# Gate and up projections as seven half-size block products in place of eight, their two 258-column chunks alternating matmul by matmul

## The chip, the cores and the metric

The kernel runs on one core of a Trainium2 chip. The metric is the device time of one execution in microseconds (us), the median of three runs. TensorE (PE) multiplies matrices; PEld are its weight loads. VectorE (DVE), ScalarE (ACT) and GpSimd (POOL) work on tiles in SBUF, DVE and ACT also on the PSUM banks that PE writes, and SyncE (SP) issues DMAs. Engines run by themselves and wait for each other by semaphores.

## The reference, cut to what matters

One decoder layer: 1024 prompt rows behind 16 meta rows and 8 sample rows go through a mixer (attention and a gated linear recurrence), then through the feed-forward part that the change touches. D_MODEL is 1024, D_FF is 2816, float32 throughout.

```
def _ffn(x, w_gate, w_up, w_down, g, b):
    hdn = jax.nn.silu(x @ w_gate) * (x @ w_up)
    return _layer_norm(ALPHA * x + hdn @ w_down, g, b)
```

The meta rows are not among the outputs of the layer, so the feed-forward part runs over 1032 columns (tokens).

## The kernel before

Activations lie transposed: features on the 128 partitions, tokens along the columns. Every product in full precision is made of three passes: a float32 value is held as a high part (fp32r) and a low part (the rest), and high weights times high columns, high times low and low times high are summed in PSUM. x1, the input of the feed-forward part, lies in `xh` and `xl` as 8 tiles of 128 features.

**Groups.** D_FF is cut into 11 groups (`FGROUPS`) of 256 hidden rows, that is two units of 128. Per group six weight panels of 128 x 1024 come by DMA into `raw`: gate and up for unit 0, gate and up for unit 1 (`job` with panels p to p+3), and two for the down product. POOL splits each panel into `wh` (a cast, L733) and `wl` (a subtraction, L735); three panel slots rotate, and a slot may be overwritten when PE begins the next panel (`panel_used`).

**Products.** `job` (L794 to L798) makes one unit of gate or up: three chunks of 344 columns (`BODY`), each in a PSUM bank of its own, 8 feature tiles x 3 passes = 24 matmuls a chunk, 72 a unit, 288 a group. ACT applies SiLU to the gate (L1831) into `sg`, DVE multiplies it by the up product (`hidden`, L2457), ACT copies the result into its high part `hh` (L1837), DVE makes the low part `hl` (L2461). `down` (L1350 to L1355) then adds the group's share of the output: 3 chunks x 8 output tiles x 2 units x 3 passes = 144 matmuls, and DVE adds each of the 24 results into `mixed` (L2489). PE runs the groups one after the other in program order; groups 1 to 9 are a loop, and group 0 (its chunks laid between the end of the first layer norm) and the last group are written out.

**The last group.** It makes its output token by token: `turn_y` transposes `mixed` for a tile of tokens (8 transposes, L1396), ACT copies it out (`y_copy`, L1875), `y_tile` adds the last group's down product for that tile with 512 columns of weights as the moving side (L1420 to L1422), and then DVE sums and takes the moments (`moments`, L2504 to L2509), ACT centres and scales (`deviation`, `centre`, L1886), POOL multiplies by the gain (L754) and, for the first three tiles, adds the shift (L758); DVE shifts the others (`shift`, L2526). Nine turns stand behind chunks of the last group's products, and tiles 0 to 3 of nine are made between its last products. SP loads gain and shift when all nine tiles are copied, and stores each tile when it is shifted; the last store ends the kernel.

Of the kernel before, what the change touches and what calls it, by code (L numbers as in the profile page):

```python
# [14 lines left out]
P = 128  # L15
# [49 lines left out]
PANELS = PAN_FFN + 6 * FGROUPS  # L65
# [163 lines left out]
FFN_PER = [5, 5, 5, 5, 5, 5, 3, 3]  # L229
# [10 lines left out]
GATE_LAST, UP_LAST = [0, 2, 4], [1, 3, 5]  # L240
Y_PAIR = [0, 6, 2, 0, 6, 4, 2, 0, 6]
# [8 lines left out]


def chunk_of(token):
    return next(c for c, (c0, cw) in enumerate(BODY) if token < c0 + cw)
# [8 lines left out]
def build(nc, IN, OUT):  # L262
    es = ExitStack()
    with es:
# [129 lines left out]
        mixed = c("mixed", [P, KT, T])  # L394
        sgb = c("sgb", [P, T])
        ysum = nc.alloc_sbuf_tensor_at("ysum", [P, T], F32, offset=R1 + KT * T * 4)
# [4 lines left out]
        z = region(OHB, 16 * T * 4)  # L401
        hh, hl = z("hh", [P, 2, T], F32R), z("hl", [P, 2, T], F32R)
        sg, hf = z("sg", [P, 2, T]), z("hf", [P, 2, 352])

        wh_end = nc.alloc_sbuf_tensor_at("wh_end", [P, D], F32R, offset=OHB + 2 * size([P, 2, T], F32))
        wl_end = nc.alloc_sbuf_tensor_at("wl_end", [P, D], F32R, offset=R1 + KT * T * 4)
        YTOK = OHB + size([P, 6, T], F32) + size([P, 2, 352], F32)
        y = region(YTOK, OHB + 16 * T * 4 - YTOK)
        ytok, ystat = y("ytok", [P, NT, D]), y("ystat", [P, NT, 12])
        ymv, ysd, yms = y("ymv", [P, NT, 2]), y("ysd", [P, NT]), y("yms", [P, NT])  # L410
        gbc = nc.alloc_sbuf_tensor_at("gbc", [P, 2, D], F32, offset=R1)
# [8 lines left out]
        def wt(buf, slot, k):  # L420
            return buf[:, slot, k * P:(k + 1) * P]

# [19 lines left out]
        def _(sp):  # L442
# [27 lines left out]
            for t in range(NT):  # L470
                rows = P if t < 8 else TAIL + NB
                if t == 0:
                    sp.dma_start(xstage[0:META, 0, :], IN["meta"]).then_inc(sem("x_loaded0"), 16)
                    sp.dma_start(xstage[META:P, 0, :], IN["x_prompt"][0, 0:P - META, :])\
                        .then_inc(sem("x_loaded0"), 16)
                elif t < 8:
                    sp.dma_start(xstage[:, t, :], IN["x_prompt"][0, P * t - META:P * t + P - META, :])\
                        .then_inc(sem(f"x_loaded{t}"), 16)
                else:
                    sp.dma_start(xlast[0:TAIL, :], IN["x_prompt"][0, SEQ - TAIL:SEQ, :])\  # L480
                        .then_inc(sem("x_loaded8"), 16)
                    sp.dma_start(xlast[TAIL:TAIL + NB, :], IN["x_sample"][:, 0, :])\
                        .then_inc(sem("x_loaded8"), 16)
# [178 lines left out]
            with sp.Fori(0, FGROUPS) as g:  # L662
                for m in range(4):
                    panel_free(PAN_FFN + 6 * g + m)
                    columns(m % RING, IN["w_up" if m % 2 else "w_gate"][0], 2 * P * g + P * (m // 2))
                for m in range(2):
                    panel_free(PAN_FFN + 6 * g + 4 + m)
                    slot = (4 + m) % RING
                    dst = raw[:, slot, :].rearrange("p (k n) -> p k n", k=2)
                    src = IN["w_down"][0][bass.ds(2 * P * g, 2 * P), :].rearrange("(k p) n -> p k n", p=P)  # L670
                    halves(slot, [(dst[:, k, :], src[:, k, 512 * m:512 * m + 512]) for k in range(2)])
# [15 lines left out]
        def _(pool):  # L687
# [51 lines left out]
            with pool.Fori(27 // RING, PANELS // RING - 1) as i:  # L739
                for s in range(RING):  # L740
                    split(s, i + raw_use(27 + s) - 27 // RING, RING * i + s, RING * i + s - RING)
            for p in range(PANELS - RING, PANELS - 1):
                split(p % RING, raw_use(p), p, p - RING)
            p = PANELS - 1
            pool.wait_ge(raw_loaded[p % RING], 32 * raw_use(p))
            pool.wait_ge(sem("hidden"), 6 * (FGROUPS - 1) + 3)
            pool.tensor_copy(wh_end[:, :], raw[:, p % RING, :]).then_inc(sem("panel_high"), 1)
            pool.wait_ge(sem("panel_high"), PANELS)
            pool.tensor_tensor(wl_end[:, :], raw[:, p % RING, :], f(wh_end[:, :]), ALU.subtract)\
                .then_inc(sem("panel_split"), 1)  # L750
# [12 lines left out]
        def _(pe):  # L763
# [46 lines left out]
            for t in range(NT):  # L810
                rows = P if t < 8 else TAIL + NB
                pe.wait_ge(sem(f"x_loaded{t}"), 32 if t in (0, 8) else 16)
# [524 lines left out]
            def down(g, p):  # L1337
                pe.wait_ge(sem("panel_split"), p + 5)
                pe.wait_ge(sem("panel_split"), p + 6)
                for c, (c0, cw) in enumerate(BODY):  # L1340
                    pe.wait_ge(sem("hidden_split"), 6 * g + 4 + c)
                    for m in range(KT):
# [3 lines left out]
                        for k in range(2):  # L1346
                            w = tuple(x[:, slot, k * 512 + (m % 4) * P:k * 512 + (m % 4 + 1) * P] for x in (wh, wl))
                            x = [x[:, k, c0:c0 + cw] for x in (hh, hl)]
# [26 lines left out]
            with pe.Fori(0, FGROUPS - 2) as g:  # L1375
                B.loop(g, FFN_PER)
                p = PAN_FFN + 6 + 6 * g
                job(p, 0, A3, ALL8, X8, chunks=BODY)
                job(p + 1, 1, B3, ALL8, X8, chunks=BODY)
                job(p + 2, 2, A3, ALL8, X8, chunks=BODY)  # L1380
                job(p + 3, 0, B3, ALL8, X8, chunks=BODY)
                down(g + 1, p)
                B.end(FGROUPS - 2)


            summed = [B.before(b) for b in range(8)]

            def turn_y(i):
                t0, w = Y_TILES[i]
                if i == 0:  # L1390
                    for b in range(8):
                        pe.wait_ge(bank_free[b], summed[b])
                else:
# [5 lines left out]
            p = PAN_FFN + 6 * (FGROUPS - 1)  # L1399
            job(p, 0, A3, ALL8, X8, after=turn_y, chunks=BODY)  # L1400
            job(p + 1, 1, B3, ALL8, X8, after=lambda c: turn_y(c + 3), chunks=BODY)

            def y_tile(i):
                t0, w = Y_TILES[i]
                b, ahead_ = Y_PAIR[i], pair_ahead(i)
                if b == 6 and ahead_ is None:
                    pe.wait_ge(sem("y_copied"), NT)
                elif ahead_ is None:
                    settled(b)
# [1167 lines left out]
```

## Time and profile before

| | us |
|---|---|
| median of 3 runs (1814.51 to 1818.33) | 1817.17 |
| profiled execution, span from first to last instruction | 1820.0 |
| PE busy in it | 1761.5 (97%) |
| DVE / ACT / POOL busy in it | 703.3 / 371.5 / 513.6 |

The profile is of one execution; the rows name a line of the kernel, an engine, what is written from what, and the shape. Two matmuls of PE overlap in the records (each lasts about twice its distance to the next), so the rate of PE is read from starts, not from durations. The feed-forward part begins at about 1041 us, group 0's down product at 1089 us, the last group at 1722 us.

### The profile page before, as it was taken

To read this page: it belongs to the slowest core of one execution; us is meant where nothing else is said; L and a number is where in the kernel's file an instruction comes from. 1 tells how busy PE (TensorE), PEld (TensorE's weight loads), DVE (VectorE), ACT (ScalarE), POOL (GpSimd) and SP (SyncE) were. 2 spreads that over 40 slices of the span, in tenths; PEclk is the share of its full clock that TensorE was granted. 3 is DMA by queue.
4 is the path that set the end of the run, shared out by engine and by line. 5 is a ranking of instruction groups with operands and counts; after the bars stand their busy time and mean duration, and the time that the engine had idled before them with its cause. 6 is when DMAs were issued, how large, how long until landed. Compare 5 with 4: busy or idle time off the path is not lost.

```text
span 1820.0 us, 29093 instructions
## 1 busy us (share of the span) xinstructions
PE 1761.5 (97%) x11328; PEld 1615.3 (89%) x11328; DVE 703.3 (39%) x1255; ACT 371.5 (20%) x699; POOL 513.6 (28%) x296
## 2 busy tenths in 40 slices
PE   7999999998999999999999999999999999999995
PEld 6967677776877879999999899999999999999994
DVE  4156767541335261111174833313312312322327
ACT  4133232322233231111120640010010010010033
POOL 4210111110212023333353823333333333333325
PEclk9899999998998889999999999999999999999998
DMA  5144434304641122111112211111111111111102
GB/s 158 59 112 131 124 116 145 117 12 128 191 135 27 47 50 56 47 46 46 47 47 58 82 47 47 47 46 46 46 46 46 46 46 47 51 45 48 50 25 93
DMA packets 175297, 127.54 MB, mean 70 GB/s; under 512 B 22362, under 2 KB 148730, under 8 KB 175218
## 3 DMA queue, kind: packets, MB, share of 16 engines
q1 hardware_dynamic: 169586, 125.12, 23.3%
q10 hardware_dynamic: 5632, 1.35, 0.5%
q8 instruction: 52, 0.85, 0.2%
q14 instruction: 27, 0.22, 0.0%
HBM read 116.57 MB, written 9.87 MB: 69 GB/s over the span
## 4 chain that ended last, share of the span: by engine, by line
PE 85%; DVE 7%; DMA 2%; ACT 2%; issue 2%; SPq 2%; POOL 0%; DVEq 0%; ACTq 0%; POOLq 0%
PE psum L794 13%; PE psum L798 13%; PE psum L797 13%; PE psum L1355 4%; PE psum L1354 4%; PE psum L1350 4%; PE psum L855 4%; PE psum L859 4%; PE psum L861 4%; PE psum L1010 3%; PE psum L1303 2%; PE psum L1307 2%; PE psum L1306 2%; PE psum L983 2%; PE psum L939 1%
## 5 line engine op out<-in xcount | busy, mean ns | idle before, releaser
L733 POOL CAST wh<-raw 128x1024 fp32r<-128x1024 f32 x131 | 145.8, 1113 | 1258.9 <-PE psum L855 389.4
L794 PE MATMUL psum<-xh,wh 128*128 128x344 f32 (+1 forms) x1392 | 449.0, 323 | 3.6 <-POOL wl L735 3.4
L797 PE MATMUL psum<-xl,wh 128*128 128x344 f32 (+1 forms) x1392 | 446.2, 321 | 0.0
L798 PE MATMUL psum<-xh,wl 128*128 128x344 f32 (+1 forms) x1392 | 446.2, 321 | 0.0
L735 POOL TENSOR_TENSOR wl<-raw,wh 128x1024 fp32r<-128x1024 f32 x131 | 333.3, 2545 | 10.5
L794 PEld LDWEIGHTS psum<-xh,wh 128*128 128x128 f32 x1392 | 263.5, 189 | 5.3 <-issue 5.3
L797 PEld LDWEIGHTS psum<-xl,wh 128*128 128x128 f32 x1392 | 263.5, 189 | 0.5 <-issue 0.5
L798 PEld LDWEIGHTS psum<-xh,wl 128*128 128x128 f32 x1392 | 263.3, 189 | 0.0
L2457 DVE TENSOR_TENSOR hf<-sg,psum 128x344 f32<-128x344 f32 x66 | 33.8, 513 | 372.8 <-PE psum L798 363.7
L855 PE MATMUL psum<-xh,wh 128*128 128x352 f32 (+1 forms) x480 | 162.8, 339 | 1.5 <-DVE ql L1992 1.5
L859 PE MATMUL psum<-xl,wh 128*128 128x352 f32 (+1 forms) x480 | 161.1, 336 | 0.0
L861 PE MATMUL psum<-xh,wl 128*128 128x352 f32 (+1 forms) x480 | 159.9, 333 | 0.0
L1355 PE MATMUL psum<-hh,wl 128*128 128x344 f32 x480 | 154.0, 321 | 0.0
L1350 PE MATMUL psum<-hh,wh 128*128 128x344 f32 x480 | 153.6, 320 | 0.0
L1354 PE MATMUL psum<-hl,wh 128*128 128x344 f32 x480 | 153.3, 319 | 0.0
L2489 DVE TENSOR_TENSOR mixed<-mixed,psum 128x344 f32<-128x344 f32 x216 | 109.9, 512 | 84.3 <-PE psum L1355 84.3
L1831 ACT ACTIVATE sg<-psum 128x344 f32<-128x344 f32 x66 | 30.1, 458 | 414.9 <-PE psum L798 401.6
L855 PEld LDWEIGHTS psum<-xh,wh 128*128 128x128 f32 x480 | 93.5, 195 | 12.0 <-issue 11.8
L859 PEld LDWEIGHTS psum<-xl,wh 128*128 128x128 f32 x480 | 93.3, 194 | 11.7 <-issue 11.7
L861 PEld LDWEIGHTS psum<-xh,wl 128*128 128x128 f32 x480 | 93.1, 194 | 10.1 <-issue 10.0
L2022 DVE CUSTOM_DVE_ANT_0 psum<-psum,cb 128x512 f32<-128x512 f32 (+5 forms) x120 | 63.6, 571 | 75.5 <-PE psum L943 42.5
L1570 ACT ACTIVATE pt<-psum,negc_tok 128x272 f32<-128x272 f32 (+3 forms) x144 | 61.3, 476 | 150.0 <-PE psum L986 78.8
(332 smaller groups left out, 2702.7 us busy)
## 6 DMA issues: line engine op xcount, KB each, us to landing
raw<-in_w_in SPq DMA_DIRECT2D x86, 256.0 KB, 3.3
parts<-in_cache_k SPq DMA_DIRECT2D x64, 256.0 KB, 3.0
parts<-in_cache_v SPq DMA_DIRECT2D x64, 256.0 KB, 2.9
raw<-in_w_gate SPq DMA_DIRECT2D x44, 256.0 KB, 3.1
raw<-in_w_up SPq DMA_DIRECT2D x44, 256.0 KB, 3.1
raw<-in_w_down SPq DMA_DIRECT2D x44, 256.0 KB, 2.7
raw<-in_w_o SPq DMA_DIRECT2D x28, 256.0 KB, 3.1
cb<-negc_scratch SPq DMA_DIRECT2D x8, 520.0 KB, 5.4
```

Of the source, the lines that this page charges most:

```text
L733: pool.tensor_copy(wh[:, s, :], raw[:, r, :]).then_inc(sem("panel_high"), 1)
L735: pool.tensor_tensor(wl[:, s, :], raw[:, r, :], f(wh[:, s, :]), ALU.subtract)\
L794: first = mm(out, w[0], x[0], start=(n == 0), stop=False)
L797: mm(out, w[0], x[1], start=False, stop=False)
L798: last = mm(out, w[1], x[0], start=False, stop=(n == len(ks) - 1))
L855: ins = mm(out, wt(wh, slot, k), xh[:, k, c0:c0 + cw], start=(k == 0), stop=False)
L859: mm(out, wt(wh, slot, k), xl[:, k, c0:c0 + cw], start=False, stop=False)
L861: ins = mm(out, wt(wl, slot, k), xh[:, k, c0:c0 + cw], start=False, stop=(k == 7))
L1350: first = mm(out, w[0], x[0], start=(k == 0), stop=False)
L1354: mm(out, w[0], x[1], start=False, stop=False)
L1355: last = mm(out, w[1], x[0], start=False, stop=(k == 1))
L2489: read(b, ve.tensor_tensor(y, y, psum[:, b, 0:cw], ALU.add))
```

## The change

Groups 1 to 10 (group 0 stays as it was) make gate and up by another formula. A group's gate product is a 2 x 2 block product: the weights in quarters of 128 hidden rows by 512 features, a (row 0, first half of the features), b (row 0, second half), c_ and d (row 1), and x1 in quarters of 512 features by 516 tokens. Eight quarter products are replaced by seven, of which four take sums of quarters:

- POOL makes from the raw quarters S1 = c + d, S3 = a - c, S2 = S1 - a and S4 = b - S2, and splits the seven units a, S1, S3, S2, b, d, S4 into high and low as before, now 128 x 512 each, six slots rotating (`room`: unit g waits until PE has done unit g - 6).
- Four sums of x1 quarters are made once, behind group 0's products: `t_make` and `t_low` on DVE, `t_high` on ACT, each 128 x 2064. They lie in `th` and `tl`; the fourth replaces a part of `xh` and `xl`.
- PE runs seven products (`seven`) for gate and seven for up. Each has 4 feature tiles x 3 passes x 2 chunks of 258 columns = 24 matmuls, into two PSUM banks that alternate. A12, A22 and S4 add onto what lies in the banks of A11, S3 and S1.
- ACT copies the banks of A11 and S1 out first (`snaps`); DVE adds the pieces (`combine`) and from them come the four blocks of 128 x 516 of gate and of up. ACT applies SiLU, DVE multiplies (`hid`), ACT makes the high part (`hid_high`), DVE the low one (`hid_low`). The hidden value takes the place of the gate in `sg`; the low part lies in the same place.
- `down_new` keeps 3 chunks of 344 and 144 matmuls. Its first chunk waits for three of the four low blocks. In its last chunk PE waits twice (`bank_full`) for its own matmuls to end before it tells POOL that a unit is done.
- In the last group turns 0 to 5 stand inside the up job's last three products, the other three beside `y_tile` 0 and 1; all nine tiles are made behind the last product.
- The loop of groups 1 to 9 is written out. SP loads quarters and half panels of 256 KB, each when the split that read its place is done.

The core of the diff:

```diff
+A11, S1, S3, S2, A12, A22, S4 = range(7)
+BANKS_OF = {A11: 0, A12: 0, S1: 2, S4: 2, S3: 4, A22: 4, S2: 6}
+DOWN_BANKS = [6, 7, 0, 1, 4, 5, 2, 3]
...
+            def unit_from(g, source):
+                high, lower = unit_of(wh, g), unit_of(wl, g)
+                step(pool.tensor_copy(high, source))
+                pool.tensor_tensor(lower, source, f(high), ALU.subtract).then_inc(sem("panel_split"), 1)
...
+                    room(g + S1)
+                    s1 = unit_of(wlf, g + S1)
+                    step(pool.tensor_tensor(s1, c_, d, ALU.add))
+                    step(pool.tensor_tensor(c_, a, c_, ALU.subtract))
+                    step(pool.tensor_tensor(a, s1, a, ALU.subtract))
+                    unit_from(g + S1, s1)
+                    room(g + S3)
+                    unit_from(g + S3, c_)
...
+                b, begins = BANKS_OF[v], v in (A11, S1, S3, S2)
+                wH, wL = unit_of(wh, g), unit_of(wl, g)
+                for k in range(4):
+                    cols = slice(k * P, k * P + P)
+                    for w, part in ((wH, 0), (wH, 1), (wL, 0)):
+                        for c in range(2):
+                            last = mm(psum[:, b + c, 0:CW], w[:, cols], moving(v, k, c)[part],
+                                      start=(begins and k == 0 and w is wH and part == 0),
+                                      stop=(k == 3 and w is wL), skip_group_check=True)
...
+                pe.wait_ge(sem("snapped"), 2 * j + 1)
+                product(n, job_, A12, turns)
+                if n == 1 and job_ == 0:
+                    pe.wait_ge(sem("x1_split"), 6 + 4)
+                pe.wait_ge(sem("combined"), 4 * j + 2)
+                product(n, job_, A22, turns)
+                pe.wait_ge(sem("snapped"), 2 * j + 2)
+                product(n, job_, S4, turns)
...
+                for c, (c0, cw) in enumerate(BODY):
+                    pe.wait_ge(sem("hidden_split"), 6 + 4 * (n - 1) + (3 if c == 0 else 4))
...
+                            last = mm(out, w[0], x[1], start=False, stop=(k == 1))
+                            if c == 2 and m % 4 == 3 and k == 0:
+                                last.then_inc(sem("unit_done"), 1)
+                        give(b, last)
+                        if c == 2 and m % 4 == 3:
+                            pe.wait_ge(bank_full[b], B.before(b))
+                            pe.sem_inc(sem("unit_done"), 1)
...
+            for n in range(3):
+                t_make(n)
+            t_low(0)
+            t_low(1)
...
+                product_done(n, job_, A22)
+                combine(n, job_, 2, c21, c12, 4)
+                if job_:
+                    dve.wait_ge(sem("combined"), 4 * j + 3)
+                    dve.wait_ge(sem("gate_rest"), 3 * (n - 1) + 2)
+                    hid(block(1, 0), c21)
+                    hid_low(n, 1)
+                    hid_low(n, 2)
...
+            def hid(g_, u_):
+                ve.tensor_tensor(g_, g_, u_, ALU.mult).then_inc(sem("hidden"), 1)
...
+                dve.wait_ge(sem("hidden_high"), 6 + 4 * (n - 1) + x + 1)
+                ve.tensor_tensor(hl[:, u, cols], sg[:, u, cols], f(hh[:, u, cols]), ALU.subtract)\
+                    .then_inc(sem("hidden_split"), 1)
...
+            seven(FGROUPS - 1, 0)
+            seven(FGROUPS - 1, up, turn_y)
+            pe.wait_ge(sem("panel_split"), PANELS + UNITS_A_GROUP * (FGROUPS - 1))
+            turn_y()
             y_tile(0)
+            turn_y()
             y_tile(1)
-            unit(0, UP_LAST[1], 1, (xh, xl))
-            unit(2, GATE_LAST[2], 2, (xh, xl))
-            y_tile(2)
-            y_tile(3)
-            unit(0, UP_LAST[2], 2, (xh, xl))
-            for i in range(4, NT):
+            turn_y()
+            for i in range(2, NT):
```

Three places in the order of the instructions, the semaphores that each instruction waits for in brackets.

TensorE, in the gate and up stage of a group of the loop. Before, the start of one chunk of a unit (`xh`, `xl` the split input, `wh`, `wl` the split weights):

```order
L794 MATMUL psum<-xh,wh 128x344 [waits bank_free3,panel_split]
L797 MATMUL psum<-xl,wh 128x344
L798 MATMUL psum<-xh,wl 128x344
L794 MATMUL psum<-xh,wh 128x344
L797 MATMUL psum<-xl,wh 128x344
L798 MATMUL psum<-xh,wl 128x344
```

Of the change, the end of product A22 of the up job, product S4 up to its second feature tile (x2 are the two chunks):

```order
L1527 MATMUL psum<-xh,wl 128x258 x2
L1527 MATMUL psum<-xh,wh 128x258 x2
L1527 MATMUL psum<-xl,wh 128x258 x2
L1527 MATMUL psum<-xh,wl 128x258 x2
L1527 MATMUL psum<-xh,wh 128x258 [waits panel_split,snapped]
L1527 MATMUL psum<-xh,wh 128x258
L1527 MATMUL psum<-xl,wh 128x258 x2
L1527 MATMUL psum<-xh,wl 128x258 x2
```

The same weights are now used by two matmuls in a row, on 258 columns each in place of 344; the sequence of high and low is the same, and each product waits for what an earlier piece of its bank was read for.

GpSimd, the weights. Before, the body of the loop, a rotation of three panels:

```order
L733 CAST wh<-raw 128x1024 [waits panel_used]
L734 REGISTER_ALU
L735 TENSOR_TENSOR wl<-raw,wh 128x1024 [waits panel_high]
L726 ISA
L728 REGISTER_ALU [waits raw_loaded1]
L733 CAST wh<-raw 128x1024 [waits panel_used]
L734 REGISTER_ALU
L735 TENSOR_TENSOR wl<-raw,wh 128x1024 [waits panel_high]
L733 CAST wh<-raw 128x1024 [waits raw_loaded2,panel_used]
L734 REGISTER_ALU
L735 TENSOR_TENSOR wl<-raw,wh 128x1024 [waits panel_high]
```

Of the change, the last down unit of group 1 and the first two units of group 2's gate job (`wlf` is the place of a low part, seen as float32, where a sum is made):

```order
L837 CAST wh<-raw 128x512 [waits unit_done,arrived4]
L838 TENSOR_TENSOR wl<-raw,wh 128x512 [waits made]
L837 CAST wh<-raw 128x512 [waits unit_done,arrived0]
L838 TENSOR_TENSOR wl<-raw,wh 128x512 [waits made]
L855 TENSOR_TENSOR wlf<-raw 128x512 [waits unit_done,arrived2,arrived1]
L856 TENSOR_TENSOR raw<-raw 128x512 [waits made]
L857 TENSOR_TENSOR raw<-wlf,raw 128x512 [waits made]
L837 CAST wh<-wlf 128x512 [waits made]
L838 TENSOR_TENSOR wl<-wlf,wh 128x512 [waits made]
```

Between the cast and the subtraction of a panel, which are now half as wide, three sums stand ahead of S1. The first two units of the next group wait for `unit_done` of the running group, that is for its up products A22 and S4.

VectorE, from the up job's first pieces to the start of the down product. Before, the hidden values of the last unit of group 0 (those of the loop read alike):

```order
L2457 TENSOR_TENSOR hf<-sg,psum 128x344 [waits bank_full3,bank_free0]
L2461 TENSOR_TENSOR hl<-hf,hh 128x344 [waits hidden_high]
L2457 TENSOR_TENSOR hf<-sg,psum 128x344 [waits bank_full4,bank_free1]
L2461 TENSOR_TENSOR hl<-hf,hh 128x344 [waits hidden_high]
L2457 TENSOR_TENSOR hf<-sg,psum 128x344 [waits bank_full5,bank_free2]
L2461 TENSOR_TENSOR hl<-hf,hh 128x344 [waits hidden_high]
L2474 SCALAR_TENSOR_TENSOR mixed<-mixed,psum 128x344 [waits bank_full6]
```

Of the change, group 1, `ub` holding the up blocks:

```order
L2790 TENSOR_TENSOR ub<-ub 128x516 [waits snapped,combined]
L2819 TENSOR_TENSOR sg<-sg,ub 128x516 [waits gate_rest,c22_ready]
L2797 TENSOR_TENSOR sg<-sg,psum 128x516 [waits first_read,unit_done]
L2826 TENSOR_TENSOR hl<-sg,hh 128x516 [waits hidden,hidden_high]
L2778 TENSOR_TENSOR ub<-ub,psum 128x516 [waits unit_done]
L2819 TENSOR_TENSOR sg<-sg,ub 128x516 [waits gate_rest,combined]
L2826 TENSOR_TENSOR hl<-sg,hh 128x516 [waits hidden_high] x2
L2778 TENSOR_TENSOR ub<-ub,psum 128x516 [waits unit_done]
L2819 TENSOR_TENSOR sg<-sg,ub 128x516 [waits gate_rest,combined]
L2826 TENSOR_TENSOR hl<-sg,hh 128x516 [waits hidden_high]
L2839 TENSOR_TENSOR mixed<-mixed,psum 128x344 [waits bank_full6]
```

Where a hidden value took the up product from PSUM, three of four now take it from `ub` in SBUF (L2819). The third low block of L2826 is the one that the down product's first chunk waits for.

## Rows read from the trace of the kernel before

**Rows 1.** The page, busy time of each engine.
```profile
PE 1761.5 (97%) x11328; PEld 1615.3 (89%) x11328; DVE 703.3 (39%) x1255; ACT 371.5 (20%) x699; POOL 513.6 (28%) x296
```

**Rows 2.** One line of the down product: count, durations, first and last start.
```profile
L1350 PE MATMUL psum<-hh,wh x480: 316/321/324, 1089.0 to 1721.7; 128*128 128x344 f32 x160
```

**Rows 3.** Timeline of TensorE: start, duration (us), instruction; four widths, three stretches.
```profile
52.13 0.25 PE L877 MATMUL psum<-xh,wl 128*128 128x8 f32 x1
...
54.14 0.25 PE L877 MATMUL psum<-xh,wl 128*128 128x8 f32 x1
...
217.22 0.29 PE L983 MATMUL psum<-ql,kh 64*128 64x256 f32 x2
...
217.45 0.29 PE L986 MATMUL psum<-nmT,onesr 64*128 64x256 f32 x2
...
227.01 0.29 PE L983 MATMUL psum<-ql,kh 64*128 64x272 f32 x2
...
227.26 0.29 PE L986 MATMUL psum<-nmT,onesr 64*128 64x272 f32 x2
...
1764.10 0.39 PE L1421 MATMUL psum<-wh,hl 128*128 128x512 f32 x1
...
1769.20 0.40 PE L1422 MATMUL psum<-wl_end,hh 128*128 128x512 f32 x1
```

**Rows 4.** Timeline of VectorE and TensorE where one waited for the other.
```profile
1774.55 2.42 DVE L2461 TENSOR_TENSOR hl<-hf,hh 128x344 fp32r<-128x344 f32 x1 [0.56 <-ACT hh L1837]
1776.81 0.31 PE L1307 MATMUL psum<-xh,wl 128*128 128x344 f32 x1
1777.11 0.47 PE L1420 MATMUL psum<-wh,hh 128*128 128x512 f32 x1
1777.42 0.40 PE L1421 MATMUL psum<-wh,hl 128*128 128x512 f32 x1
```

**Rows 5.** Timeline of VectorE and ScalarE, one hidden chunk in the loop.
```profile
1262.60 0.51 DVE L2457 TENSOR_TENSOR hf<-sg,psum 128x344 f32<-128x344 f32 x1 [14.54 <-PE psum L798]
1263.14 0.49 ACT L1837 ACTIVATE hh<-hf 128x344 fp32r<-128x344 f32 x1 [3.85 <-DVE hf L2457]
1263.67 0.52 DVE L2461 TENSOR_TENSOR hl<-hf,hh 128x344 fp32r<-128x344 f32 x1 [0.56 <-ACT hh L1837]
```

**Rows 6.** Timeline of GpSimd in the loop.
```profile
1259.12 1.04 POOL L733 CAST wh<-raw 128x1024 fp32r<-128x1024 f32 x1 [7.79 <-PE psum L794]
1260.25 2.40 POOL L735 TENSOR_TENSOR wl<-raw,wh 128x1024 fp32r<-128x1024 f32 x1
```

**Rows 7.** Groups by line and shape: a short cast (busy us, mean ns).
```profile
L715 POOL CAST identr<-ident 128x128 fp32r<-128x128 f32 x1 | 0.3, 291 | 0.1
```

**Rows 8.** The chain of waits: start, duration, ScalarE copy of 1376 columns.
```profile
1065.16 1.36 ACT xh L1825
```

**Rows 9.** Timeline of GpSimd and VectorE side by side before the feed-forward part.
```profile
1015.33 3.58 POOL L735 TENSOR_TENSOR wl<-raw,wh 128x1024 fp32r<-128x1024 f32 x1
1017.15 2.14 DVE L2386 TENSOR_TENSOR ysum<-ysum,mixed 128x344 f32<-128x344 f32 x1
```

**Rows 10.** Timeline of GpSimd during group 0.
```profile
1075.71 2.78 POOL L735 TENSOR_TENSOR wl<-raw,wh 128x1024 fp32r<-128x1024 f32 x1
```

**Rows 11.** Timeline of the last group.
```profile
1722.33 0.51 DVE L2489 TENSOR_TENSOR mixed<-mixed,psum 128x344 f32<-128x344 f32 x1 [0.43 <-PE psum L1355]
...
1774.19 2.40 POOL L754 TENSOR_TENSOR ytok<-ytok,gbc 128x1024 f32<-128x1024 f32 x1 [16.42 <-ACT ytok L1886]
...
1802.43 1.20 DVE L2504 TENSOR_TENSOR ytok<-ytok,psum 128x1024 f32<-128x1024 f32 x1
...
1806.52 1.20 DVE L2504 TENSOR_TENSOR ytok<-ytok,psum 128x1024 f32<-128x1024 f32 x1
```

**Rows 12.** The chain of waits: one turn of eight transposes.
```profile
1726.07 0.87 PE psum L1396 x8
```

**Rows 13.** DMA issues: count, KB each, us to landing.
```profile
gbc<-in_ln_b SPq DMA_DIRECT2D x1, 512.0 KB, 4.8
```

More of the change, by code:

```diff
@@ L661, in _ @@
                 columns((PAN_O + n) % RING, IN["w_o"][0], P * (n % 8))
[L662 to L671, printed above, removed]
+            for m in range(4):
+                panel_free(PAN_FFN + m)
+                columns(m % RING, IN["w_up" if m % 2 else "w_gate"][0], P * (m // 2))
@@ L746, in _, with step @@
[L746 to L750, printed above, removed]
+            steps = [14]
+            def step(ins):
+                steps[0] += 1
+                ins.then_inc(made, 1)
+                pool.wait_ge(made, steps[0])
@@ L1374, in _, with moving @@
             down(0, p)
[L1375 to L1383, printed above, removed]
+            up = 1
+            def moving(v, k, c):
+                low_, high = META + CW * c, META + TH + CW * c
+                if v == A11:
+                    return xh[:, k, low_:low_ + CW], xl[:, k, low_:low_ + CW]
+                if v == A12:
+                    return xh[:, 4 + k, low_:low_ + CW], xl[:, 4 + k, low_:low_ + CW]
+                if v == S4:
+                    return xh[:, 4 + k, high:high + CW], xl[:, 4 + k, high:high + CW]
+                if v == A22:
+                    return xh[:, k, high:high + CW], xl[:, k, high:high + CW]
+                t = {S1: 0, S3: 1, S2: 2}[v]
+                return th[:, t, k, CW * c:CW * c + CW], tl[:, t, k, CW * c:CW * c + CW]
@@ new lines, in hid_high @@
+            def hid_high(n, x):
+                u, h = ((1, 1), (0, 0), (1, 0), (0, 1))[x]
+                act.wait_ge(sem("hidden"), 6 + 4 * (n - 1) + x + 1)
+                do(hh[:, u, TH * h:TH * h + TH], block(u, h), ACT.Copy).then_inc(sem("hidden_high"), 1)
+            for n in range(1, FGROUPS - 1):
+                snaps(n, 0)
+                gate_silus(n)
+                snaps(n, 1)
+                for x in range(4):
+                    hid_high(n, x)
+            snaps(FGROUPS - 1, 0)
@@ L1872, in y_copy @@
+            gate_silus(FGROUPS - 1)
+            snaps(FGROUPS - 1, 1)
             def y_copy(i):
@@ L2491, in _ @@
                     settled(b)
-                B.end(FGROUPS - 2)
-            skip(A3)
-            for c in range(3):
-                hidden(FGROUPS - 1, 0, c)
             def moments(i):
```

457 lines of the change are left out of this document (331 added, 126 removed).

## The prediction

> **What bounds the kernel now.** I read the page's busy times first: PE is busy for 1761.5 of the 1820.0 us span [rows 1], so the time is PE's, and what counts is the distance from one matmul to the next and every wait that PE does not have now. Then the first and last start of the down product's line in groups 0 to 9: 1089.0 and 1721.7 us [rows 2]. Between them lie nine whole groups of 432 matmuls and one down product up to its third last matmul, 9 x 432 + 141 = 4029 distances in 632.7 us, that is 157.0 ns each, the waits in it included. At 344 columns nothing stands still: a group is 432 x 157.0 = 67.8 us, of which gate and up take 288 x 157.0 = 45.2 and down 22.6.
>
> **Price of a matmul on 258 columns.** No row has it. Its neighbours, from starts [rows 3]: 8 columns, 18 distances in 2.01 us, 112 ns (from there on a narrower matmul gains nothing); 256 columns, 2 in 0.23 us, 115; 272 columns, 2 in 0.25, 125; 512 columns, 22 in 5.10, 232. A line from 512 through 344 (157) falls by 0.445 ns a column and gives 118.7 at 258; one from 344 through 272 gives 119; 256 itself gives 115. I take 118.5, with ends 112 (the floor) and 125 (the 272 row as it stands). The 256 and 272 rows use 64 partitions, two at a time; that all 128 cost the same is my choice, since 344 columns lie on the same line. Two PSUM banks in turn are in the 256 and 272 rows too.
>
> The Trainium skill, "TensorE: Matmul & The Clock Gate", section "Back-to-back issue gap", puts an isolated matmul's distance at N / 2.4 + 2.5 ns. By that 258 columns would be 110 and 344 columns 146; the trace has 157 and differs, so the sum does not use it; what 110 would make is a rival below.
>
> **The loop, groups 1 to 9.** Gate and up: 14 products x 24 = 336 matmuls x 118.5 = 39.8 us in place of 45.2, a gain of 5.4. Down stays at 22.6. Three things come back.
>
> First, PE waits twice a group for its own matmul to end. A matmul's record lasts 0.31 us from its start [rows 4], 0.15 beyond its turn; after a wait the next started 0.14 us behind the releaser (VectorE's end at 1774.55 + 2.42 = 1776.97 to 1777.11), and its successor came 0.31 behind it where 0.23 is normal [rows 3, 4]. That is 0.15 + 0.14 + 0.08 = 0.4, twice 0.8 us. Ends: 0.2 and 1.5.
>
> Second, the hidden blocks. Now down's first chunk waits for blocks that came out of PE two chunks earlier (48 x 157.0 = 7.5 us); then it waits for the block of A22, with only S4 (24 x 118.5 = 2.84 us) between. Durations at 516 columns: DVE 0.51 at 344 and 1.20 at 1024 [rows 5, 11] give 0.69; ACT 0.49 at 344 and 1.36 at 1376 [rows 5, 8] give 0.63; handing on costs 0.04 (1262.60 + 0.51 to 1263.14 and so on [rows 5]). From A22's last turn: 0.2 until it ends, combine 0.69, multiply 0.69, ACT's high part 0.63, low part 0.69, four handings 0.16, restart of PE 0.2: 3.3 us against 2.84, late by 0.4.
>
> But VectorE and GpSimd stand in each other's way. A DVE operation on 344 columns with both inputs in SBUF, 0.52 us alone [rows 5], took 2.14 and 2.42 us beside a POOL instruction and ended 0.38 us after it both times [rows 4, 9, 11]; the first of these POOL instructions took 3.58 in place of 2.40 [rows 6, 9]. So each waits for the other's whole instruction, and after it the other goes. The multiply and both low parts of this chain have both inputs in SBUF. POOL is there at just this time: its next units wait for the end of A22 and of S4, as the order above shows. A POOL cast of 512 columns is 0.61 (0.29 at 128, 1.04 at 1024 [rows 6, 7]), a sum or subtraction, with the cast's fixed 0.18, 1.29, of which 1.11 shuts VectorE out; VectorE's stream of 0.54 shuts POOL out. With A22's last turn as zero: its end at 0.2 releases DVE's combine and POOL's cast; the multiply streams from 1.07 to 1.62, POOL's subtraction to 2.73, the first low part to 3.27; S4's end at 3.04 has released POOL's first sum, which streams to 4.38; the second low part ends at 4.92, PE goes on at 5.2. Late by 2.4 us where down could start at 2.84. Ends: 0.4 (POOL never in the way) and 4.3 (all three wait for a whole 1.29).
>
> The Trainium skill, "GPSIMD Engine Reference", section "8. Key points", says that GpSimd shares its SBUF interfaces with VectorE and that it contends with VectorE instructions with two SBUF inputs. The trace agrees: 2.14 us for 0.52. By that rule the move of up blocks from PSUM into `ub` exposes the multiply too; without it the wait would be 0.4 and the result rival 1's.
>
> Third, POOL's weights. A group needs 18 casts, 18 subtractions and 8 sums: 18 x 0.61 + 26 x 1.29 = 44.5, with gaps of 0.08 [rows 6] 48 us of a 65 us group, against 6 x 3.5 = 21 now. Units come 2 us apart (S1 6 us), PE eats one in 2.84, and six slots let POOL work ahead from the last down units on. I cost it at nothing beside the chain above: PE's 22.6 us of down, in which only four units are used, hide it. If POOL were a third slower that cover would be gone.
>
> The other new waits are covered: A22 waits for two combines, 0.2 + 1.5 us, behind A12's 2.84; S1 of the up job for one, behind A11's 2.84.
>
> Group of the loop: 39.8 + 22.6 + 0.8 + 2.4 = 65.6, gain 2.2 us, nine times 20.
>
> **Group 0.** The four sums of x1 quarters are 2064 columns: 2.30 us on DVE, of which 2.15 shut POOL out. Three makes and two low parts stand in VectorE's queue in front of the second unit's hidden values, behind which down 0 waits. VectorE is free at 1076.2, POOL's subtraction runs to 1078.5 [rows 10], and a cast and a subtraction of the last panel (0.9 and 2.2 of stream) come between: 1078.5 + 3 x 2.2 + 3.1 + 2 x 2.3 = 1092.8, then multiply, copy and low part of 344 columns 1.6: down starts at 1094.4 in place of 1089.0, 5.4 late. The other make and low parts delay the reading of PSUM by about as much as down 0 allows; I add 0.6. Cost 6, ends 0 (PE finds cover) and 9.
>
> **Last group.** Now from 1722.1 (the last read less its 0.2) to 1820.0: 97.9 us. After: products 39.8, six turns of 0.87 [rows 12] make 45.0; three more turns, two tiles of 12 x 0.232 = 2.8, and about 2.5 of waits for the last block and for ACT's copies: the ninth copy is out at 56. Only then the gain and shift load, 4.8 us [rows 13]: POOL starts at 61, where now it starts at 1774.2, that is 52 [rows 11]. Seven POOL instructions of 2.48 stand before VectorE's first shift: 78.4. From there a shift of 1.2 and two rounds of 4.1 (1802.43 to 1806.52) to the last tile's moments, 87.8, and from these to the end as now, 13.5 us [rows 11]: 101. So the shorter products are eaten here, because no tile is made between them any more: +3, ends -3 and +6.
>
> **Sum.** -20 + 6 + 3 = -11 on the profiled 1820.0: 1809. That execution stands 2.8 us above the median of 1817.2; from the median it is 1806.
>
> **Rivals.**
> 1. VectorE's chain slips past POOL (PE is late by 0.4 only): the loop gains 4.2, -38 + 9 = -29, 1788. For it: POOL's two releases come only just ahead of VectorE's. Against: a POOL instruction is longer than the room between VectorE's. Chance 0.13.
> 2. The chain loses every turn: late by 4.3 or more at the start of each down product, the loop gains 0.3, -3 + 9 = +6, 1823, slower. It decides from 3.4 us on, where 9 x (4.6 - 3.4) is used up by the 9 of group 0 and the last one. For it: low part 0 and the first multiply can also meet POOL; against: the chain above has POOL at its worst in two of three places. Chance 0.15.
> 3. 258 columns cost 125 ns as 272 did: 3360 x 6.5 = 22 us back, 1828, slower. Against: the lines through 344. Chance 0.08.
> 4. They cost 112 or less, the floor of the 8-column row: 3360 x 6.5 = 22 us more, 1784. For it: 256 at 115; against: the lines through 344. Chance 0.10. The skill's 110 of the section named above would make it 1777.
> 5. POOL cannot feed PE: it waits for units in every group, above 1830. Chance 0.04.
>
> **How the numbers follow.** The forecast has 0.50, and its own range, from late 1.5 to 3.2, is 1798 to 1814. What a measurement of this kernel can tell from no change is 0.2%, 3.6 us. Faster: forecast 0.46, rivals 1 and 4 0.23, together 0.69. Slower: most of 2, 3, 5, 0.20. Same 0.11. The range of 8 in 10 leaves out 5, the far end of 4 and most of 3: 1782 to 1826.
>
> **What would show it.** Right: L1527's starts 118 or 119 ns apart; PE's idle time in the loop mainly ahead of L1587's first matmul, some 2.4 us nine times, put down to VectorE's low part L2826, whose mean is well above 0.69; down 0's first start 5 to 6 us after the last chunk; POOL's first gain about 61 us into the last group. Wrong: L1527 above 122; idle PE behind POOL's units; L2826 at 0.69, which is rival 1.

## The result and the profile after

The changed kernel takes 1829.23 us (median of 5 runs, 1823.61 to 1831.73), 1.0065 times the kernel before, with a 95% interval of 1.0046 to 1.0083. It is slower by some 12 us; forecast was 1806, faster by 11. The forecast missed by 23 us. The profiled execution has a span of 1828.0 us, to be held against the 1820.0 of before. PE has 480 matmuls more and is 32.5 us less busy than in [rows 1]:

```profile
PE 1729.0 (95%) x11808; PEld 1579.7 (86%) x11808; DVE 824.2 (45%) x1323; ACT 392.1 (21%) x701; POOL 769.7 (42%) x616
```

So the matmuls did become cheaper, and what was gained stands idle or went elsewhere. By stretches, from starts on PE (before from [rows 2, 11]):

| us | before | forecast | after |
|---|---|---|---|
| up to the last gate or up matmul of group 0 | 1088.8 | 1088.8 | 1083.6 |
| from there to group 1 | 22.8 | 28.8 | 30.0 |
| groups 1 to 9 | 610.4 | 590 | 608.9 |
| last group, to the end | 97.8 | 101 | 105.5 |

The first line is no effect of the change: among the profiled kernels below that have the same code there, that matmul starts between 1081 and 1092 us. Most of the miss is in the loop, which should have given 20 us and gave 1.6.

The waits of PE from 1075 us on (total, times, longest, in us) stand where they were forecast:

```profile
PE psum L1587 <- DVE hl L2826: 18.4, 9, 2.0
PE psum L1475 <- DVE hl L2711: 5.2, 1, 5.2
PE psum L1527 <- PE psum L1589: 2.7, 9, 0.3
```

L1587 is the first matmul of a new down product and L2826 VectorE's low part, L1475 is group 0's down product, L1527 behind L1589 the wait of PE for its own matmul, seen at the end of down only. The timeline of group 1 (start, duration, instruction) shows the first of these waits and what comes after it:

```profile
1152.19 0.69 DVE L2819 TENSOR_TENSOR sg<-sg,ub 128x516 f32<-128x516 f32 x1
...
1152.26 1.78 POOL L838 TENSOR_TENSOR wl<-raw,wh 128x512 fp32r<-128x512 f32 x1
...
1152.81 3.49 DVE L2826 TENSOR_TENSOR hl<-sg,hh 128x516 fp32r<-128x516 f32 x2
...
1153.91 0.40 PE L1527 MATMUL psum<-xh,wl 128*128 128x258 f32 x2
1154.48 1.26 POOL L855 TENSOR_TENSOR wlf<-raw 128x512 f32<-128x512 f32 x1 [0.44 <-PE psum L1527]
...
1156.35 0.43 PE L1587 MATMUL psum<-hh,wh 128*128 128x344 f32 x1 [2.04 <-DVE hl L2826]
1156.61 0.32 PE L1588 MATMUL psum<-hh,wl 128*128 128x344 f32 x1
...
1157.71 0.36 PE L1589 MATMUL psum<-hl,wh 128*128 128x344 f32 x1
1157.87 0.49 PE L1587 MATMUL psum<-hh,wh 128*128 128x344 f32 x1
1158.15 0.49 PE L1588 MATMUL psum<-hh,wl 128*128 128x344 f32 x1
...
1161.02 0.44 PE L1589 MATMUL psum<-hl,wh 128*128 128x344 f32 x1
1161.30 0.33 PE L1587 MATMUL psum<-hh,wh 128*128 128x344 f32 x1
```

Up to 1156.61 this is the forecast: POOL's subtraction and sum stand between VectorE's steps, two low parts need 3.49 us, PE goes on 2.3 us behind the start of its last product matmul. Then comes what no step had: from 1157.87 to 1161.30 twelve matmuls follow each other at 0.286 us in place of 0.157. 12 x 0.13 = 1.5 us are lost after the wait has ended. The view by stretches (length, PE busy, granted clock, then the share and the GB/s of DMA) shows what it is, one row per down product with what separates it from the next group, groups 1, 2, 3 and 9, then group 0:

```profile
1156.35:1181.56 25.21, 24.76 (x145) 0.93 0.04 11
1224.32:1248.05 23.73, 23.27 (x145) 1.00 0.04 12
1290.82:1316.05 25.23, 24.77 (x145) 0.93 0.04 11
...
1698.79:1722.52 23.73, 23.27 (x145) 1.00 0.04 12
1089.13:1113.66 24.53, 24.53 (x144) 0.92 0.01 2
```

At a mean of 0.93 part of the stretch ran at 0.50, the lower level of 1.2 GHz. Seven of the nine groups have 0.93 and 25.2 us, two have 1.00 and 23.7. So a loop group takes 68.0 or 66.5 us, where 67.8 was before and 65.6 forecast.

The last group's chain (start, duration) goes over the load of gain and shift and POOL:

```profile
1779.53 6.57 DMA gbc<-in_ln_b
...
1786.17 2.42 POOL ytok L879
```

At its end VectorE's first shift stands beside one more POOL instruction and takes 3.27 us, where the next one takes 1.20 (timeline):

```profile
1803.04 3.27 DVE L2872 TENSOR_TENSOR ytok<-ytok,gbc 128x1024 f32<-128x1024 f32 x1 [10.03 <-POOL ytok L879]
...
1809.20 1.20 DVE L2872 TENSOR_TENSOR ytok<-ytok,gbc 128x1024 f32<-128x1024 f32 x1
```

### The profile page after: what moved, and what is told of

The parts are those of the page before. It is cut to its first block, busy times and chain, and to the rows that moved or that the text cites. A ratio compares the mean times of both kernels' runs of the same rounds, so it can differ in the third digit from the quotient of the medians.

```text
span 1828.0 us, 29515 instructions
## 1 busy us (share of the span) xinstructions
PE 1729.0 (95%) x11808; PEld 1579.7 (86%) x11808; DVE 824.2 (45%) x1323; ACT 392.1 (21%) x701; POOL 769.7 (42%) x616
## 4 chain that ended last, share of the span: by engine, by line
PE 82%; DVE 10%; issue 2%; DMA 2%; ACT 2%; POOL 1%; SPq 1%; DVEq 0%; ACTq 0%; POOLq 0%
PE psum L1527 21%; PE psum L919 5%; PE psum L922 5%; PE psum L923 5%; PE psum L1587 4%; PE psum L1589 4%; PE psum L1588 4%; PE psum L980 4%; PE psum L984 4%; PE psum L986 4%; PE psum L1135 3%; PE psum L1108 2%; PE psum L1428 2%; PE psum L1432 2%; PE psum L1431 2%
## 5 line engine op out<-in xcount | busy, mean ns | idle before, releaser
L811 POOL TENSOR_TENSOR wl<-raw,wh 128x1024 fp32r<-128x1024 f32 x72 | 191.1, 2654 | 5.8
L838 POOL TENSOR_TENSOR wl<-raw,wh 128x512 fp32r<-128x512 f32 x140 | 185.2, 1323 | 11.2
L1587 PE MATMUL psum<-hh,wh 128*128 128x344 f32 x432 | 144.7, 335 | 19.7 <-DVE hl L2826 18.4
L919 PE MATMUL psum<-xh,wh 128*128 128x344 f32 (+1 forms) x480 | 156.4, 326 | 4.8 <-POOL wl L811 3.4
L923 PE MATMUL psum<-xh,wl 128*128 128x344 f32 (+1 forms) x480 | 155.2, 323 | 0.0
L922 PE MATMUL psum<-xl,wh 128*128 128x344 f32 (+1 forms) x480 | 155.1, 323 | 0.0
L1589 PE MATMUL psum<-hl,wh 128*128 128x344 f32 x432 | 142.9, 331 | 0.0
L1527 PE MATMUL psum<-xh,wh 128*128 128x258 f32 x640 | 130.4, 285 | 2.7 <-PE psum L1589 2.7
L1527 PE MATMUL psum<-xh,wl 128*128 128x258 f32 x640 | 129.1, 283 | 0.0
L1527 PE MATMUL psum<-xl,wh 128*128 128x258 f32 x640 | 129.1, 283 | 0.0
L1587 PEld LDWEIGHTS psum<-hh,wh 128*128 128x128 f32 x432 | 85.1, 197 | 23.9 <-DVE hl L2826 20.2
L980 PEld LDWEIGHTS psum<-xh,wh 128*128 128x128 f32 x480 | 93.3, 194 | 12.0 <-issue 11.8
L1527 PEld LDWEIGHTS psum<-xh,wh 128*128 128x128 f32 x640 | 99.1, 189 | 5.0 <-issue 5.0
L984 PEld LDWEIGHTS psum<-xl,wh 128*128 128x128 f32 x480 | 93.0, 194 | 11.7 <-issue 11.7
```

The costliest lines, as they stand in the source:

```text
L811: pool.tensor_tensor(wl[:, s, :], raw[:, r, :], f(wh[:, s, :]), ALU.subtract)\
L838: pool.tensor_tensor(lower, source, f(high), ALU.subtract).then_inc(sem("panel_split"), 1)
L919: first = mm(out, w[0], x[0], start=(n == 0), stop=False)
L922: mm(out, w[0], x[1], start=False, stop=False)
L923: last = mm(out, w[1], x[0], start=False, stop=(n == len(ks) - 1))
L980: ins = mm(out, wt(wh, slot, k), xh[:, k, c0:c0 + cw], start=(k == 0), stop=False)
```

## The experiments

**The idle time filled.**

```diff
+                    if c == 0:
+                        pe.wait_ge(sem("combined"), 4 * j + 1)
+                        for _ in range(18):
+                            mm(psum[:, 6, 0:CW], xh[:, 0, META:META + P], xh[:, 0, META:META + CW], ...)
                     pe.wait_ge(sem("hidden_split"), 6 + 4 * (n - 1) + (3 if c == 0 else 4))
```

> The changed kernel, with 18 matmuls of 258 columns whose result nobody reads laid ahead of each of the nine new down products, into PSUM bank 6, which stands empty there: 18 x 0.12 = 2.2 us, as long as PE waits at this place in the changed kernel. The wait stays, PE is only not idle in it. Theory 1 (the granted clock falls to its lower level because PE stands idle): no stretch of lower clock in the loop, the down product takes 23.1 us in all nine groups in place of 24.6 in seven of them, 7 x 1.5 = 10.5 us less, 1829 to 1818.5. Rival (the matmuls at double distance after the wait have another cause, such as POOL's or VectorE's traffic): the stretch stays and the time stays at 1829, or rises by what the extra matmuls run over the wait, at most 9 x 0.3.

Measured: 1816.59 us (12 runs), 1.0001 times the kernel before (0.9988 to 1.0014). From the timeline of group 1, and the stretch of its down product with the filling:

```profile
1152.56 2.32 PE L1575 MATMUL psum<-xh 128*128 128x258 f32 x18
1154.79 0.43 PE L1592 MATMUL psum<-hh,wh 128*128 128x344 f32 x1
```
```profile
1152.56:1178.51 25.95, 25.50 (x165) 1.00 0.04 11
```

All nine stretches have 1.00. Down starts no earlier than in the changed kernel, 2.36 us behind the last product matmul, and yet 12.6 us are gone. By the traces 10.3 of them lie in the loop, where 10.5 were expected; the last group is 1.6 us shorter, since its load took 4.87 us in that execution in place of 6.57. The lower clock comes from PE's standing idle, not from the traffic around it.

**Half of it filled.** The same with `range(9)`.

> The changed kernel with 9 matmuls laid ahead of each of the nine down products where an earlier run had 18: they cover 1.1 of the 2.2 us, so that PE still stands idle for 1.1 us. Theory (only a long enough wait brings the lower clock): no matmuls at double distance in the loop, a group of 66.5 us, 1818 as with 18. Rival (any wait of this size brings it, or the wait and not its length): still 1.5 us in most of the groups, 1827 to 1830.

Measured: 1817.98 us (12 runs), 0.9998 (0.9986 to 1.001). The waits of PE, and the stretch of group 1's down product:

```profile
PE psum L1592 <- DVE hl L2831: 8.8, 9, 1.0
```
```profile
1157.93:1181.66 23.73, 23.27 (x145) 1.00 0.04 12
```

PE stands idle for 1.0 us nine times, each group takes 66.5 us, and no matmul of these nine groups runs at double distance. So a wait of 2.04 us had a price beyond itself, one of 1.0 had not.

**POOL out of VectorE's way.**

```diff
                     come(n, ha, 0)
+                    if n > 1 and job_ == 0:
+                        pool.wait_ge(sem("hidden_split"), 6 + 4 * (n - 1))
                     room(g + A11)
```

> The changed kernel, with one wait more on POOL: it begins the next group's units only when the last low part of this group's hidden blocks is done, so that none of its instructions stands beside VectorE's chain ahead of down. Theory 1 (the wait of 2.2 us ahead of down is VectorE and POOL shutting each other out, and the clock falls because of the wait): the low parts come down from 1.74 us each to 0.69, PE's wait to 0.4 us, the clock holds in the loop: 9 x 1.8 + 10.5 = 27 us less, 1829 to 1802. Rival A (the chain is as long without POOL): the wait stays at 2 us, the time at 1829. Rival B (POOL, some 2.5 us later, becomes late with its weights): the wait ahead of down goes, but PE waits for POOL's units in the next group, up to 2.5 us a group, and the time is 1820 or more.

Measured: 1800.18 us (6 runs), 0.9902 (0.9885 to 0.9919). The low part over all groups, who waits for it, and the two ahead of group 1's down product:

```profile
L2828 DVE TENSOR_TENSOR hl<-sg,hh x40: 685/696/1637, 1152.0 to 1744.0; 128x516 fp32r<-128x516 f32 x40
...
  PEld psum L1589: 2.2, 9
```
```profile
1155.01 1.48 DVE L2828 TENSOR_TENSOR hl<-sg,hh 128x516 fp32r<-128x516 f32 x2
```

PEld are PE's weight loads. The median low part is 0.70 us, where it was 1.64, and the two ahead of down took 1.48 us in place of 3.49. From the last product matmul to down's first there are 0.32 us, of which 0.12 is a normal turn: PE's wait is down to 0.2 us, POOL is not late with its units, and a group takes 64.5 us at full clock. The chain and its price were right, and one line gives 29 us, of which by the traces 18 are the waits and 10.5 the clock.

**The wait alone, in the kernel before.**

```diff
-                    pe.wait_ge(sem("hidden_split"), 6 * g + 4 + c)
+                    pe.wait_ge(sem("hidden_split"), 6 * g + 6)
```

> The kernel before, with one edit: all three chunks of its down product wait for the hidden values of the last chunk, where each waited for its own. Down so begins one multiply, copy and low part of 344 columns after the last chunk's matmul: 0.2 + 0.5 + 0.5 + 0.5 and handing on, about 2.0 us of idle PE in each of ten groups, without quarters, block products or POOL beside it. Theory 1 (a wait of this length brings the granted clock down for the start of down): 10 x (2.0 + 1.5) = 35 us more, 1817 to 1852, with matmuls at twice the distance in down. Rival (the lower clock belongs to the changed kernel's other load): only the waits, 10 x 2.0, 1837, and no stretch of lower clock.

Measured: 1847.96 us (4 runs), 1.0175 (1.0152 to 1.0198). Ahead of down, and its stretches in groups 0, 1, 2 and 8:

```profile
PE psum L1350 <- DVE hl L2461: 18.4, 10, 1.9
```
```profile
1082.65:1105.42 22.77, 22.77 (x144) 1.00 0.08 24
1152.54:1176.89 24.35, 24.35 (x145) 0.93 0.08 23
1224.01:1248.37 24.36, 24.36 (x144) 0.93 0.07 22
1652.84:1675.66 22.82, 22.82 (x144) 1.00 0.08 23
```

A wait of 1.9 us is enough in the old kernel too. Seven of ten groups have the lower clock: 10 x 2.0 + 7 x 1.55 = 31 us, 30 measured. That the rest keep theirs had not been expected, hence 1848 and not 1852.

**The chunks one after the other.**

```diff
-                for k in range(4):
+                for c, k in [(c, k) for c in range(2) for k in range(4)]:
```

> The changed kernel, with the two chunks of a product one after the other, 12 matmuls into one PSUM bank and then 12 into the next, in place of alternating matmul by matmul. The number of matmuls and weight loads is the same. Theory 1 (a matmul's distance is set by its columns alone): 120 to 121 ns as now, 1829 within 3 us. Rival A (two banks in turn are what makes 258 columns cheap, or two equal weights in a row are): the distance rises, by 5 ns 3360 x 5 = 17 us, 1846. Rival B (the change of bank at each matmul is what makes 120.7 of the 118.5 forecast): 118.5, 7 us less, 1822.

Measured: 1823.7 us (13 runs), 1.0031 (1.002 to 1.0042). A group's products in this kernel, first and last start, 335 distances in 40.23 us:

```profile
1188.51 0.36 PE L1527 MATMUL psum<-xh,wh 128*128 128x258 f32 x1 [0.30 <-PE psum L1589]
...
1228.74 0.28 PE L1527 MATMUL psum<-xh,wl 128*128 128x258 f32 x1
```

and in the changed kernel, 334 distances in 40.32 us:

```profile
1181.56 0.48 PE L1527 MATMUL psum<-xh,wh 128*128 128x258 f32 x2 [0.30 <-PE psum L1589]
...
1221.88 0.40 PE L1527 MATMUL psum<-xh,wl 128*128 128x258 f32 x2
```

120.1 ns against 120.7. Alternating costs 0.6 ns, 2 us in all, as part of rival B had it; it gains nothing. The 5.5 us between the medians are more than that. In the profiled execution, the slowest of the 13, six of nine groups have the lower clock, one less than above, at 1.5 us each; the rest is not explained.

**The changed kernel again.**

> The changed kernel once more, to stand beside the three others of this set. Nothing is left out or altered. Expected 1829 as before, with the start of down at the lower clock in most of the nine groups; it tells how far the time moves from execution to execution, since the lower clock comes in some groups and not in others, at 1.5 us each.

Measured: 1830.79 us (6 runs, 1827.65 to 1834.54), 1.0066 (1.0044 to 1.0089). Again seven of nine groups have the lower clock, but others: the first and the eighth are free of it here, the second and the ninth in the first profile.

**No wait of PE for its own matmuls.**

```diff
-                        if c == 2 and m % 4 == 3:
-                            pe.wait_ge(bank_full[b], B.before(b))
-                            pe.sem_inc(sem("unit_done"), 1)
...
+                            if (c, m, k) == (2, 4, 0):
+                                first.then_inc(sem("unit_done"), 1)
...
+                            if n > 1 and job_ == 0 and v == A11 and c == 0 and k == 0 and w is wH and part == 0:
+                                last.then_inc(sem("unit_done"), 1)
```

> The kernel in which POOL waits for the last low part (1800 us), and in which PE no longer waits twice a group for its own matmul to end: the two signals to POOL that a unit is done are given by the next matmul, down's first of output tile 4 and the first of the next group. Theory 1 (the two waits cost what the trace shows over an undisturbed sequence: 23.07 us for 143 distances of 0.157, so 0.6, and 0.62 in place of 0.16 at the end, 0.46): 9 x 1.06 = 9.5 us less, 1790.5. Rival (behind each of these waits PE would wait anyway, for a bank or a unit of POOL): the time stays at 1800, and the idle time goes over to another releaser.

Measured: 1788.92 us (6 runs), 0.9838 (0.9814 to 0.9862). The end of group 1, where the changed kernel had 0.63 us between these two starts (1180.93 to 1181.56):

```profile
1175.83 0.32 PE L1595 MATMUL psum<-hl,wh 128*128 128x344 f32 x1
1175.99 0.40 PE L1529 MATMUL psum<-xh,wh 128*128 128x258 f32 x2
```

A group takes 63.5 in place of 64.5 us, 9 us in nine groups. No other wait took its place. The medians differ by 11.3; the last group is 1.8 us shorter in this trace, since its load took 4.71 us in place of 6.42, which the edit does not touch.

**Group 0.**

```diff
-            t_low(0)
-            t_low(1)
             skip(A3)
...
-                if c < 2:
-                    t_low(2 + c)
+                t_low(c)
+            t_low(3)
```

> The kernel in which POOL waits for the last low part (1800 us), and in which the first two low parts of the sums of x1 quarters no longer stand in VectorE's queue ahead of group 0's last hidden values, but behind the reads of down 0's first and second chunk (the other two behind the third). Theory 1 (5.4 us of wait ahead of down 0, of which these two low parts of 2.2 each make 4.4, and the lower clock behind it, which makes down 0 24.9 us where it was 22.6): down 0 starts about 1 us behind the last product and holds its clock, 4.4 + 2.3 = 6.7 us less, 1793.5. Rival (the low parts then hold up the reading of PSUM, or come too late for the second product of group 1): PE waits in down 0 or ahead of that product, and of the 6.7 us less than half is left, 1797 or more.

Measured: 1792.09 us (6 runs), 0.9864 (0.9842 to 0.9887). The waits of PE:

```profile
PE psum L1589 <- DVE hl L2826: 1.4, 1, 1.4
...
PE psum L1477 <- DVE hl L2713: 0.7, 1, 0.7
```

Down 0 waits 0.7 us in place of 5.2 and takes 22.6 us in place of 24.9. From group 0's last product to group 1 there are 23.85 us where 30.56 were, the 6.7 expected. The rival has a grain of truth: the first new down product waits 1.4 us more, since VectorE is behind, so that 5.3 us are left in the trace.

**Gain and shift loaded early.**

```diff
-        gbc = nc.alloc_sbuf_tensor_at("gbc", [P, 2, D], F32, offset=MIXED)
+        gbc = y("gbc", [P, 2, D])
...
-            sp.wait_ge(sem("y_copied"), NT)
+            sp.wait_ge(sem("unit_done"), unit_no(FGROUPS - 1, 1, S2) + 1)
```

> The kernel in which POOL waits for the last low part (1800 us), and in which gain and shift have a place of their own, in the space of the x1 sums, and are loaded when the last group's third-last product begins, not when the ninth tile is copied. Theory 1 (the chain of the last group runs from the ninth copy over the load of 6.6 us to POOL's seven instructions and VectorE behind them): POOL's first gain follows the first centred tile, 3 to 4 us earlier, and the end comes as much earlier, 1796.5. Rival (VectorE's nine sums and moments are what sets the end): POOL starts earlier, but the end stays, 1800.

Measured: 1795.35 us (6 runs), 0.988 (0.9858 to 0.9901). POOL's gains in this kernel, what they wait for, and who waits for them:

```profile
L881 POOL TENSOR_TENSOR ytok<-ytok,gbc x8: 2335/2342/2421, 1751.8 to 1784.6; 128x1024 f32<-128x1024 f32 x7, 8x1024 f32<-8x1024 f32 x1
...
  ACT ytok L2147: 31.1, 4
...
  DVE ytok L2874: 6.6, 1
```

The load no longer releases it. The first gain is 60.1 us into the last group (1751.8 less 1691.7) where it was 63.5, and the last group takes 102.0 in place of 105.4. VectorE now waits 6.6 us for POOL.

**The four together.** POOL's wait and the last three edits in one kernel.

> The changed kernel with the four mends together: POOL begins the next group when the last low part is done, no wait of PE for its own matmuls, the low parts of the x1 sums behind the reads of down 0, gain and shift in a place of their own. If the four terms lie in different places and add up, as the single runs measured them (1800.2 less 11.3, 8.1 and 4.8): 1776. If one of them only uncovers the next wait, 1780 or more.

Measured: 1780.45 us (5 runs, 1779.73 to 1785.54), 0.9809 (0.9793 to 0.9825). Two groups, the second and the ninth:

```profile
1168.12:1231.62 63.50, 63.47 (x483) 1.00 0.17 51
1612.68:1676.19 63.51, 63.48 (x483) 1.00 0.17 50
```

PE is not idle from the loop's second group on, and this version beats both kernels. It is 4 us above the sum. The 1.4 us wait of the first new down product is still there, but it was in the run on group 0 too. From group 0's last product matmul to the end, the traces of the three single runs gain 10.2, 5.2 and 3.1 us, 18.5 together, and this one 17.3; 1.8 of the 10.2 are the shorter load of that execution, which no longer counts when the load is early. So by the traces the terms do add up, and it is the medians of the single runs that promised more.

**Two more tries on it**: chunks one after the other, and `POOL_SHIFTS = 1` in place of 3.

> The kernel with the four mends, and the two chunks of a product one after the other in place of alternating. In the first run without alternation the distance was 119.8 to 120.1 ns in place of 120.5 to 120.7; 3360 x 0.6 = 2 us less, 1774, if the shorter distance is due to the order. If it was by chance, the same time as the kernel with the four mends.

> The kernel with the four mends, in which POOL adds the shift for one tile in place of three and VectorE for the other eight. In the last group VectorE stands idle for 6.6 us until POOL's seventh instruction ends; with five instead of seven ahead of it 2 x 2.4 us go, and VectorE gets two shifts more of 1.2 us: 2.4 us less or somewhat better, 1773. Rival (VectorE's shifts each wait for a whole POOL instruction, as the chain ahead of down did, so that each costs 2.4 and more): the same or slower.

Measured: 1781.9 (1779.46 to 1783.6) and 1783.6 us (1780.52 to 1784.38), 5 runs each. Neither can be told from the kernel with four mends, whose runs cover the same range. In the traces the products do take 40.2 us a group for 40.4, and the last group 100.5 for 102.0, but the medians do not follow. Both stay undecided.

## Why the prediction was wrong

**The step that failed** is the second of the three things that come back in the loop, the hidden blocks. It priced the wait ahead of down at its own length: "late by 2.4 us where down could start at 2.84". The wait came, nine times, at 2.2 us, from the chain that was named. But after a wait of that length the chip granted the lower clock for a part of down, 1.5 us in seven of nine groups, and 1.8 behind group 0's longer wait of 5.2 us, 12.3 us in all. The filled kernels show it: the same wait without idle PE gives 10.3 us back in the loop.

A hint of it lies in the trace of before, in a place that I did not look at. The longest of PE's waits from 600 to 640 us there is this one, which ends at 623.7 us:

```profile
PE psum L831 <- ACT gvT L1680: 1.7, 1, 1.7
```

and the stretches around it are these, the second behind the wait; the third stands behind a wait of 1.9 us that ends at 642.6 us, and keeps the clock:

```profile
620.00:624.69 4.69, 2.70 (x22) 1.00 0.00 0
624.69:634.93 10.24, 9.17 (x36) 0.50 0.67 166
642.59:652.00 9.41, 8.49 (x58) 1.00 0.21 57
```

So the trace could tell that a wait of this length may bring the clock down, not how often. Nor is the first case a clean one: transposes stand around that wait, and not a row of products.

The Trainium skill, "TensorE: Matmul & The Clock Gate", section "HAM oscillation — how this bites in real kernels", says of a loop that waits for a DMA of about 3 to 5 us in every turn that TensorE falls back to the lower of its two clock levels each time, so that the price of a change of clock is paid again and again, and that the cure is a loop order that keeps TensorE supplied. The trace agrees on the fall and on the cure, with 0.93 in seven of nine groups and 1.00 in all nine when filled; but here the wait was 2.04 us, shorter than in the page's example, and two groups kept the clock. Nothing in the prediction weighed it.

The other terms, against what was measured:

- **Price of a matmul on 258 columns**: 120.7 ns, not 118.5, inside its ends; 336 x 2.2 ns x 9 = 6.7 us. 0.6 ns of it is the alternating. The line through 512 and 344 columns was too steep.
- **PE's own two waits**: 1.0 us a group, not 0.8, by the run without them; 1.8 us in all.
- **POOL's weights at nothing**: right, PE waits for no unit, even when POOL starts later.
- **Rival 1, no POOL in the way**: not what happened, but one line brings it about, 1800; it was priced at 1788. Rival 2 had the right sign and nearly the size, 1823, from the wrong mechanism: the wait was not longer, but what followed it was slow. (By its own sum it turns at 3.6 us late, not at 3.4: 9 x (4.6 - 3.6) = 9.) Rival 3 names 1828, next to the measured time, but for a distance of 125 ns; at 120.7 it is 7 us of its 22, and the nearness is luck.
- **Signs of being wrong**: none of the three was seen; the distance stayed below 122, no unit of POOL was waited for, and L2826 lay at 1.64. None of them looked at the clock.
- **Group 0**: down 0 came 5.35 us late, forecast were 5.4 and 0.6 on top. With the 1.8 us of the lower clock behind it, the cost is 7.2 where 6 were forecast.
- **Last group**: +7.6, not +3. The ninth copy was out at 56.6 us, as forecast 56; the load took 6.57 in place of 4.8 [rows 13], POOL's first gain came at 63.7, not 61. VectorE's first shift then took 3.27 us in place of 1.2, beside one more POOL instruction.

In sum: clock 12.3, columns 6.7, last group 4.6, own waits 1.8, less 1.8 for the wait ahead of down (2.2 for 2.4, nine times) and 0.6 in group 0, 23.0 us. The medians miss by 23, the three lower lines of the table by 24; of the 1 us between, 0.9 is PE's restart behind the wait, 0.26 in place of 0.157 us nine times.

## What to carry to other kernels

A wait of TensorE that comes back in a loop is to be priced with what follows it: look in the trace for waits of the same length and read the granted clock behind them; where it falls behind some and not behind others, the fall is a rival with a price and a chance. Where two engines shut each other out on a path that TensorE waits for, let the one that has time begin later; here that one line gave 29 us, and the shorter products save PE some 41 in the loop (4.6 us a group, by the starts). What a cheaper product saved here showed only when the operations between it and the next product had room.

## What the runs showed of the hardware

- Waits of 1.9 and 2.04 us were followed by matmuls at half clock in seven groups of ten and of nine (six of nine with the chunks one after the other), a wait of 1.0 us in none of nine. Which groups keep the clock changes from execution to execution of the same kernel; what decides it was not tried.
- The lower clock does not begin with the first matmul after the wait: in group 1 nine matmuls ran at 0.157 us (the first at 0.26) before twelve at 0.286.
- In the chain ahead of down, two low parts took 3.49 us with POOL beside them and 1.48 without.
